# Feed-forward, gate and up: the upper weights under upper and lower input as one stream of 512 columns

## The reference, cut to what matters

```
def swiglu(h, w_in, w_out):
    gu = h @ w_in                                   # 1024 -> 2 x 2816
    return (jax.nn.silu(gu[..., :D_FF]) * gu[..., D_FF:]) @ w_out
# in each of two layers, twice:
x = x + 0.5 * rmsnorm_2(swiglu(rmsnorm_2(x, g[0]), ffn_w_in[i, 0], ffn_w_out[i, 0]), g[1])
```

## Time and profile before

| | |
|---|---|
| median of 3 runs | 1996.78 us (1995.46 to 2007.18) |
| the profiled execution, from first to last instruction | 1997.9 us |
| TensorE busy | 1878.1 us, 94% of the span, 12914 matmuls |
| VectorE busy | 1354.4 us, 68% |
| ScalarE busy | 1103.4 us, 55% |
| gate/up matmuls, L1589 (4224) | 277.4 + 260.6 us |
| down matmuls, L1567 (2112) | 268.7 us |

### The profile page before, as it was taken

The page is one execution under the profiler, slowest core; times in us unless marked ns, Lnnn a source line. Parts: engine busy times, 40 slices in busy tenths (PEclk is TensorE's granted clock), DMA queues, the critical chain, the costliest instruction groups (busy, mean ns, idle before and its releaser), DMA issues.

```text
span 1997.9 us, 31359 instructions
## 1 busy us (share of the span) xinstructions
PE 1878.1 (94%) x12914; PEld 1665.4 (83%) x12914; DVE 1354.4 (68%) x1795; ACT 1103.4 (55%) x1625; POOL 10.3 (1%) x12
## 2 busy tenths in 40 slices
PE   7998999999999998999899899997999969899997
PEld 5887677777777777999788799997999958799997
DVE  3625999999999995655433465556677685265655
ACT  3334889888888985434333444445543362344444
POOL 0000000000000000000000000000000020000000
PEclk9999999999999999999999999999999978899998
DMA  6325899999999993554233354433598311455420
GB/s 250 127 87 202 327 369 367 349 370 351 369 364 365 361 369 142 188 190 148 78 110 129 158 195 176 176 134 127 191 93 280 113 44 48 176 195 189 174 92 21
DMA packets 56483, 409.41 MB, mean 205 GB/s; under 512 B 15360, under 2 KB 20992, under 8 KB 22160
## 3 DMA queue, kind: packets, MB, share of 16 engines
q1 hardware_dynamic: 51792, 400.51, 55.6%
q10 hardware_dynamic: 4544, 6.85, 1.1%
HBM read 406.22 MB, written 1.11 MB: 204 GB/s over the span
## 4 chain that ended last, share of the span: by engine, by line
PE 70%; DVE 25%; ACT 2%; issue 1%; DMA 0%; DVEq 0%; ACTq 0%; SPq 0%
PE wk L1589 26%; DVE ws_moe L1069 16%; PE acc L1567 13%; PE wk L378 5%; PE wk L1023 3%; PE wk L1908 3%; PE wk L384 2%; PE wk L1723 2%; PE wk L947 2%; PE acc L913 2%; PE wk L333 2%; PE acc L730 1%; PE acc L1937 1%; DVE rstd L305 1%; DVE sq L1136 1%
## 5 line engine op out<-in xcount | busy, mean ns | idle before, releaser
L1069 DVE TENSOR_TENSOR ws_moe<-ring,ws_moe 128x1024 fp32r<-128x1024 f32 x384 | 447.4, 1214 | 5.6 <-ACT ws_moe L1062 5.4
L1062 ACT ACTIVATE ws_moe<-ring 128x1024 fp32r<-128x1024 f32 x384 | 384.3, 1051 | 5.3 <-PE wk L1023 2.2
L1589 PE MATMUL wk<-hx,gu 128*128 128x256 f32 x2112 | 277.4, 290 | 4.8 <-DVE hx L1605 4.5
L1589 PEld LDWEIGHTS wk<-hx,gu 128*128 128x128 f32 x2112 | 266.0, 195 | 10.2 <-DVE hx L1605 6.7
L1023 PE MATMUL wk<-ws_moe,xp_moe 128*128 128x512 f32 x1024 | 269.5, 405 | 1.6 <-DVE xp_moe L1091 1.6
L1567 PE MATMUL acc<-hh_ffn,dn_ffn 128*128 128x256 f32 x2112 | 268.7, 284 | 2.0 <-issue 2.0
L1567 PEld LDWEIGHTS acc<-hh_ffn,dn_ffn 128*128 128x128 f32 x2112 | 261.0, 193 | 2.1 <-issue 2.1
L1589 PE MATMUL wk<-hx,gu_ffn 128*128 128x256 f32 x2112 | 260.6, 283 | 0.0
L1589 PEld LDWEIGHTS wk<-hx,gu_ffn 128*128 128x128 f32 x2112 | 256.6, 192 | 0.0
L1537 ACT ACTIVATE hT<-hT 128x256 f32<-128x256 f32 x88 | 36.8, 418 | 368.0 <-DVE hT L1622 368.0
L1023 PEld LDWEIGHTS wk<-ws_moe,xp_moe 128*128 128x128 f32 x1024 | 187.9, 189 | 43.8 <-issue 2.8
(11 more groups left out here) (355 smaller groups left out, 2356.4 us busy)
## 6 DMA issues: line engine op xcount, KB each, us to landing
ring<-in_u_moe SPq DMA_DIRECT2D x129, 1536.0 KB, 8.3
ring<-in_u_ffn SPq DMA_DIRECT2D x88, 1536.0 KB, 6.5
ring<-in_u_qkv SPq DMA_DIRECT2D x12, 1024.0 KB, 4.9
ring<-in_u_ple SPq DMA_DIRECT2D x8, 1280.0 KB, 5.6
ring<-in_u_in SPq DMA_DIRECT2D x9, 1024.0 KB, 4.8
ring<-in_u_glu SPq DMA_DIRECT2D x8, 1024.0 KB, 5.0
ring<-in_u_out SPq DMA_DIRECT2D x4, 1024.0 KB, 4.8
ring<-in_u_o SPq DMA_DIRECT2D x4, 1024.0 KB, 4.9
```

Of the source, the lines that this page charges most:

```text
L1062: e.activation(WS[:, n % NWS, 0, :], piece(x), ACT.Copy).then_inc(s.m_hi, 1)
L1069: e.tensor_tensor(WS[:, n % NWS, 1, :], piece(x), WS[:, n % NWS, 0, :].bitcast(F32), SUB).then_inc(s.m_lo, 1)
L1589: m = e.matmul(b[:, a * T:(a + 1) * T], gu_of(c, f)[:, x, a * 1024 + k * 128:a * 1024 + (k + 1) * 128], HX[:, y, k, :], start=k == 0 and a ...
```

## The change

A use of PSUM per tile becomes two, one bank for gate and one for up, always a pair of neighbours (`two`), so a use may be skipped ahead of a feed-forward. In a bank the right half takes lower weights by upper input (256 columns). The upper weights then run once under both halves of the input, 512 columns, into the whole bank: upper by upper at the left, upper by lower at the right, on top of what is there. 48 matmuls and weight loads of a tile become 32. The two halves of a bank must be added: ScalarE copies the right halves of both banks to hT (one copy of 2 x 256 columns), VectorE adds the left halves to them, and multiplies the sum, gate and up at once, by the norm's row. Before, VectorE multiplied out of PSUM. The wait for f_hl (the buffer set of two tiles before is free) goes from VectorE to ScalarE's copy.

```diff
+        def two(k):
+            assert k % 2 == 0
+            return wk[:, k % 4:k % 4 + 2, :]
...
-            K.then(("norm", ("ffn", c)), *[("u", c, f) for f in range(NF)])
+            K.then(("norm", ("ffn", c)))
+            if len(K.place) % 2:
+                K.then(("skip", c))
+            K.then(*[("u", c, f, a) for f in range(NF) for a in range(2)])
...  ffn_act
+                GU = hT[:, 3 * (f % 2):3 * (f % 2) + 2, :]
                 G_, U_, S_ = (hT[:, 3 * (f % 2) + i, :] for i in range(3))
-                e.wait_ge(s.f_g, n + 1)
+                k = K("u", c, f, 0)
+                bank_out(e, k + 1)
+                if f >= 2:
+                    e.wait_ge(s.f_hl, n - 1)
+                e.activation(GU, two(k)[:, :, T:2 * T], ACT.Copy).then_inc(s.f_c, 1)
+                bank_read(e, k + 1)
                 e.activation(S_, G_, ACT.Silu).then_inc(s.f_s, 1)
...  ffn_pe
+            skipped = ("skip", c) in K.place
+            if skipped:
+                ks = K("skip", c)
+                bank_in(e, ks)
+                e.nop().then_inc(freed[ks % 4], 1)
             for f in range(NF):
                 n = c * NF + f
-                b = bank_in(e, K("u", c, f))
+                ku = K("u", c, f, 0)
+                b = [bank_in(e, ku), bank_in(e, ku + 1)]
...
                     for a in range(2):
-                        for i, (x, y) in enumerate(THREE):
-                            m = e.matmul(b[:, a * T:(a + 1) * T], gu_of(c, f)[:, x, a * 1024 + k * 128:a * 1024 + (k + 1) * 128],
-                                         HX[:, y, k, :], start=k == 0 and a == 0 and i == 0, stop=k == 7 and i == 2, skip_group_check=True)
-                m.then_inc(s.filled, 1)
+                        w = gu_of(c, f)[:, :, a * 1024 + k * 128:a * 1024 + (k + 1) * 128]
+                        m = e.matmul(b[a][:, T:2 * T], w[:, 1, :], HX[:, 0, k, :], start=k == 0, stop=False, skip_group_check=True)
+                        if skipped and (f, k, a) == (0, 7, 0):
+                            m.then_inc(s.filled, 1)
+                        m = e.matmul(pair(b[a]), w[:, 0, :], HX[:, :, k, :], start=False, stop=k == 7, skip_group_check=True)
+                        if k == 7:
+                            m.then_inc(s.filled, 1)
...  ffn_dve
-                b = bank_out(e, k)
-                if f >= 2:
-                    e.wait_ge(s.f_hl, n - 1)
-                e.tensor_tensor(G_, b[:, 0:T], row, MUL).then_inc(s.f_g, 1)
-                e.tensor_tensor(U_, b[:, T:2 * T], row, MUL).then_inc(freed[k % 4], 1)
+                e.wait_ge(s.f_c, n + 1)
+                e.tensor_tensor(GU, two(k)[:, :, 0:T], GU, ADD).then_inc(freed[k % 4], 1)
                 bank_read(e, k)
+                e.tensor_tensor(GU, GU, bc(row, 2), MUL).then_inc(freed[(k + 1) % 4], 1)
                 e.wait_ge(s.f_s, n + 1)
```

More of the change, by code:

```diff
@@ L123 @@
     "m_last m_yl m_y m_gat m_xh m_xl m_gt m_G m_comb m_shift "
-    "f_gh f_gl f_dh f_dl f_xh f_xl f_xs f_g f_s f_p f_hh f_hl f_dn f_end "
+    "f_gh f_gl f_dh f_dl f_xh f_xl f_xs f_c f_s f_p f_hh f_hl f_dn f_end "
     "x_hi x_lo w_hi w_lo ple_s ple_y "
@@ L1491, in ffn_split_hi @@
                 if f >= 2:
-                    e.wait_ge(s.filled, K("u", c, f - 2) + 1)
+                    e.wait_ge(s.filled, K("u", c, f - 2, 1) + 1)
                 e.activation(gu_of(c, f)[:, 0, :], w[:, 0:2048], ACT.Copy).then_inc(s.f_gh, 1)
@@ L1546, in ffn_act @@
             if c % 2:
-                e.wait_ge(s.filled, K("u", c, NF - 2) + 1)
+                e.wait_ge(s.filled, K("u", c, NF - 2, 1) + 1)
                 ple_split_hi(e, c // 2, 0)
@@ L1612, in ffn_dve @@
                 n = c * NF + f
-                k = K("u", c, f)
+                k = K("u", c, f, 0)
                 if f == 0:
```

## The result

The changed kernel takes 2010.58 us (median of 5, 2008.61 to 2013.08), the kernel before 1996.78. The ratio is 1.0055, 95% interval 1.0033 to 1.0077: about 11 us, or half a per cent, slower. The medians are 13.8 us apart, which lies inside the interval (7 to 15 us). The forecast was 2004, with a range of 1995 to 2018.

What follows compares the result with a forecast made beforehand. TensorE's gate/up and down matmuls were taken to bound the kernel. Third feed-forward +11.2, three undisturbed ones -1.6 each, side gates +0.6: +7.0 us on a profiled span of 1997.9, 1.1 above the median, so 2004 us; range 1995 to 2018.

Steps and rivals of the forecast that it cites:

- The chain: In each tile, copy, add and wider multiply ahead of SiLU: 0.99 us longer on VectorE, plus 0.64 of copy.
- The third feed-forward: There VectorE's and ScalarE's cycle per tile grows from 8.35 to 9.34 us, over TensorE's 8.43: +11.2 us.
- Start and end: In each undisturbed feed-forward, +1.29 us at the start (tile 2 later) and +1.35 before the last down block.
- The saving on TensorE: Gate/up matmuls: 0.0135 us per matmul less, 0.213 us of 5.76 per tile, period 8.43 instead of 8.64.
- rival B: Gate/up streams: no saving per matmul, 2017 us; half of it (0.233 per 512-column stream) gives 2010; chance 0.15.
- The interruption: Third feed-forward before: TensorE sat 2.02 us on nothing; 3.6 us on the path, which vanish after the change.
- The sum again: Whole kernel: 11.2 - 3 x 1.6 + 0.6 = +7.0 us, forecast 2004 us.
- side gate's split: On ScalarE in feed-forwards 1 and 3 it follows, so the squares start some 0.3 us later: +0.6 for both.
- Rival A: All stages stay TensorE's and the saving comes through: 1978 us at best, 1991 with starts and ends; chance 0.08.
- rival C: ScalarE's copy, queued behind the gate/up split, puts 0.64 us on the cycle (9.98 in third feed-forward): 2017; chance 0.07.

Runs made afterwards that it cites:

- second profile of before: The kernel before, unchanged, profiled once more: span 1995.3 us, third feed-forward 195.8 us.
- run with the old scheme there alone: Changed kernel with the third feed-forward done as before the change (48 matmuls into one bank, multiplies out of PSUM): 1997.14 us, ratio 0.9996 to before.
- run with the chain alone: Changed kernel with the 48 matmuls of before and the new readers (copy, add, multiply): 2014.15 us, ratio 1.0074 to before.
- grouped run: Changed kernel, in every tile after the first the 16 streams of 256 columns first, then the 16 of 512: 2004.69 us, ratio 1.0030 to before.

## Why the prediction was right, and where not

The forecast said slower by 7 us; measured are 11 by the ratio, 13.8 between the medians, and 13.7 between the two profiles without an interruption (2009.0 and 1995.3). The mechanism is the one forecast; two terms of the sum were off and partly made up for by others. Step by step:

- **The chain.** Forecast 0.99 more on VectorE and 0.64 of copy; measured 1.46 - 0.46 = 1.00 and 0.63. Right. Left out was that the product follows SiLU sooner, 0.44 after it instead of 0.52.
- **The third feed-forward.** Forecast a cycle of 9.34 with the copy hidden; measured 9.28, the copy 3.1 us ahead of its use. Against the second profile of before the stage grew by 208.9 - 195.8 = 13.1 us; the forecast's 11.2 plus the 3.6 that it set off is 14.8, too much by 1.7. Of that 0.7 is the cycle (12 tiles, 0.06 each, which is the product's earlier start), and 0.7 lies in the first eight tiles, 71.2 us from add to add where the forecast had 71.9. There the forecast gave the whole pace to VectorE; in some of these tiles the period is TensorE's 8.52. From tile 8 on the bound moved from TensorE to the chain, which the run with the old scheme there alone confirms.
- **Start and end.** Forecast 1.29 and 1.35; measured 788.77 against 787.16, less 0.3 for a later start of the stage, so 1.3, and 1.24. Right in the sum. But the gap ahead of tile 2 was to be 1.7 and is 1.26, because tiles 0 and 1 save nothing: from the first gate/up matmul to the first down block are 16.65 us, before 16.58. The run with the chain alone shows start and end without the saving, +2.6 to +2.9.
- **The saving on TensorE: the term that was mis-sized.** I took 0.226 us for a stream of 512 from a run of equal streams and said that no row shows 256 and 512 taking turns. Taking turns, the pair takes 0.353 and not 0.3465: 0.115 us a tile and not 0.213. In three feed-forwards with 20 tiles that count, 3 x 20 x 0.098 = 5.9 us less gain. They came out at +0.2 or +0.3 each instead of -1.6. That is the half of rival B, 0.233 for a stream of 512, and the grouped run shows that it comes from the order. Its 2010 is what was measured, and in part by luck, since that sum takes the interruption out too.
- **The interruption.** I counted its 3.6 us as part of the time of before and let the change remove it. It wasn't in the next profile of before, so the forecast was too low by that, for a reason that one profile couldn't show. A hint was there: a run's time is 1.8 us more than its span (2010.58 and 2008.8, 1997.13 and 1995.3), so by the same 1.8 the profiled execution of before was 2.9 us above the median of the runs and not 1.1. I should have set the sum against a path without it.
- **The sum again.** Without the interruption the forecast was 14.8 - 4.8 + 0.6 = 10.6. The third took 1.7 less, the three others 5.5 more (+0.2 each for -1.6), and the 0.6 of the side gate's split isn't in the stages: 13.8, and the two profiles are 13.7 apart.
- **Rival A** fails with the cycle of 9.28, **rival C** with the copy's place: it would have needed the copy just ahead of the add at 1501.48, and it began at 1498.36.

What stays open is what TensorE does when a 512-column stream follows a 256-column one. By the grouped run a matmul less is worth (5.76 - 5.57)/16 = 12 ns here. The Trainium skill (TensorE: Matmul & The Clock Gate, Back-to-back issue gap) adds 2.5 ns per matmul to the time of its columns, in a formula that it gives for a matmul by itself; for a sustained stream with weight loads it has about 131 ns at 512 columns, where these step by 228. For these streams the measurement decides against both figures.

## What to carry to other kernels

Merging matmuls moves work from TensorE to the engines that read PSUM. Before that, find the engine cycle per tile in every stage that uses the code, and not in the typical one alone: a stage with side work on VectorE had 0.3 us to spare, and this one stage of four made the whole loss, while start and end ate the gain of the three others. Where a longer chain is hidden in the middle of a stream, keep the short form for its first and last tile, and put streams of equal length next to each other, at least by twos. And profile the kernel before twice before an odd gap goes into a sum.

## What the runs showed of the hardware

At a granted clock of 1.00, streams in fp32r with a weight load each step by 0.120 us (256 columns) and 0.228 (512) among their like, and an alternating pair takes 0.353. Two and two, the period of a tile is 8.453 us, nearly that of full grouping (8.447) and not halfway to alternation (8.527). A 512-column stream read as two runs of 256 costs the same as one run of 512 (period 8.53 in both). A copy from two banks (128x512, 0.597 us on average) takes what a pass over one bank took before (0.598). Two dependent 128x512 operations on VectorE start 0.72 to 0.73 us apart. Cut in halves that interleave, the operations start every 0.33 us, and SiLU, which needs only the first half, starts 1.12 us after the first add instead of 1.46.
